# Another order of the forty attention steps in the even mixer of a two-layer diffusion backbone

## The reference, cut to what matters

```python
# MLA, each of 8 heads:          p = softmax((qn kn^T + qr kr^T) * scale);  o = p v
# differential, each of 4 heads: p = softmax(q1 k1^T * s) - lam * softmax(q2 k2^T * s);  o = p v
```

## Time and profile before

| | |
|---|---|
| median of 3 runs | 2596.94 us (2593.97 to 2598.43) |
| profiled execution | 2596.0 us, span 2594.3 us |
| PE busy | 2534.3 us (98% of the span) |
| VectorE, ScalarE, POOL busy | 1666.4, 1141.7 and 932.0 us |
| attention loop, first maximum to the last step's | 677.80 to 837.82 us: 160.02 us |
| PE, VectorE, ScalarE busy in it | 141.95, 119.97 and 102.69 us |

### The profile page before, as it was taken

How to read it: one execution, slowest core, us unless ns; L and a number is a source line. 1 busy time by engine, 2 the same in 40 slices (tenths; PEclk the granted TensorE clock), 3 DMA queues, 4 the chain that set the end, 5 groups by cost and what they waited for, 6 DMA issues and landing times. The chain is left out here.

```text
span 2594.3 us, 44719 instructions
## 1 busy us (share of the span) xinstructions
PE 2534.3 (98%) x18549; PEld 2433.6 (94%) x18549; DVE 1666.4 (64%) x2596; ACT 1141.7 (44%) x1939; POOL 932.0 (36%) x646
## 2 busy tenths in 40 slices
PE   6999999999988999999999999999999999999999
PEld 5999999999766999999999999999999999999998
DVE  5865757524677677576767757676464557757484
ACT  5442424442666454333446433344432546434253
POOL 2432434443200344334344433434332224443342
PEclk8999999999999999999999999999999999999999
DMA  7334434321100223434322343432312112232222
GB/s 272 129 131 148 143 135 142 106 91 52 60 1 1 98 66 130 147 101 169 122 82 82 130 147 102 168 121 74 101 53 72 56 46 69 66 95 69 82 78 78
DMA packets 204048, 260.35 MB, mean 100 GB/s; under 512 B 4932, under 2 KB 158152, under 8 KB 203848
## 3 DMA queue, kind: packets, MB, share of 16 engines
q1 hardware_dynamic: 203176, 254.88, 29.5%
q10 hardware_dynamic: 672, 2.62, 0.3%
HBM read 253.66 MB, written 3.82 MB: 99 GB/s over the span
## 5 line engine op out<-in xcount | busy, mean ns | idle before, releaser
L2406 POOL TENSOR_TENSOR wl<-raw,wh 128x512 fp32r<-128x512 f32 x324 | 471.4, 1485 | 705.0 <-ACT wh L2496 602.2
L2496 ACT CAST wh<-raw 128x2048 fp32r<-128x2048 f32 (+1 forms) x102 | 174.0, 1706 | 318.1 <-PE psU L3167 277.1
L2435 POOL TENSOR_TENSOR wl<-wsum,wh 128x512 fp32r<-128x512 f32 x72 | 94.1, 1306 | 363.7 <-ACT wh L2572 363.7
L2837 DVE SCALAR_TENSOR_TENSOR x<-psG,hgate,x 128x128 f32<-128x128 f32 (+1 forms) x232 | 88.4, 435 | 167.0 <-PE psG L3167 167.0
L3287 PE MATMUL psG<-sum_h,wh 128*128 128x320 f32 x576 | 178.8, 310 | 1.1
L3290 PE MATMUL psG<-sum_h,wl 128*128 128x320 f32 x576 | 177.6, 308 | 0.0
L3289 PE MATMUL psU<-sum_l,wh 128*128 128x320 f32 x576 | 177.6, 308 | 0.0
L3290 PE MATMUL psU<-sum_h,wl 128*128 128x320 f32 x576 | 177.6, 308 | 0.0
L3289 PE MATMUL psG<-sum_l,wh 128*128 128x320 f32 x576 | 177.6, 308 | 0.0
L3287 PE MATMUL psU<-sum_h,wh 128*128 128x320 f32 x576 | 177.5, 308 | 0.0
L2431 POOL TENSOR_TENSOR wl<-raw,wh 128x512 fp32r<-128x512 f32 x72 | 104.4, 1450 | 202.9 <-ACT wh L2581 202.9
(11 more groups left out here) (699 smaller groups left out, 7651.8 us busy)
## 6 DMA issues: line engine op xcount, KB each, us to landing
mraw<-in_mod_w SPq DMA_DIRECT2D x64, 1024.0 KB, 7.2
raw<-in_ffn_w_gate SPq DMA_DIRECT2D x44, 1024.0 KB, 5.1
raw<-in_ffn_w_up SPq DMA_DIRECT2D x44, 1024.0 KB, 5.1
raw<-in_ffn_w_down SPq DMA_DIRECT2D x48, 768.0 KB, 4.4
raw<-in_odd_w_in SPq DMA_DIRECT2D x12, 1024.0 KB, 5.1
raw<-in_even_w_in SPq DMA_DIRECT2D x9, 1024.0 KB, 5.1
raw<-in_ffn_w_down SPq DMA_DIRECT2D x8, 1024.0 KB, 4.9
mscale<-in_mod_w SPq DMA_DIRECT2D x4, 1024.0 KB, 10.7
```

What stands on the lines that cost most here:

```text
L2406: ins = nc.gpsimd.tensor_tensor(wl[:, slot, piece], raw[:, slot, piece], wh[:, slot, piece].bitcast(F32), ALU.subtract)
L2435: nc.gpsimd.tensor_tensor(part1(f, wl, 3), part1(f, wsum, 3), part1(f, wh, 3).bitcast(F32), ALU.subtract).then_inc(block_plo, 1)
L2496: nc.scalar.copy(wh[:, slot, 0:width], raw[:, slot, 0:width]).then_inc(w_hi, 1)
L2837: ins = nc.vector.scalar_tensor_tensor(out=xt, in0=src, scalar=hg_of(i * 2 + m, c), in1=xt, op0=ALU.mult, op1=ALU.add)
```

## The change

The function group gives the order of the ten steps of one i. Its new order keeps each long step's place among its kind, and puts the two context steps of each i between long steps:

- i = 0: D0 A0 D1 A1 D4 A2 D2 A4 D3 A3
- i = 1 and 2: A0 D4 A1 D0 A2 D1 A4 D2 A3 D3
- i = 3: A0 D4 A1 D0 A4 D1 A2 D2 A3 D3

Everything that hangs on the order (places of key halves, of casts and squares, counts for semaphores) is worked out from SEQ by the same code as before. The last four steps are the same.

```diff
@@ -499,8 +499,11 @@
 
     def group(i):
         lat, dif = [("A", i, j) for j in range(5)], [("D", i, j) for j in range(5)]
-        firsts = [x for j in range(4) for x in ((lat[j], dif[j]) if i else (dif[j], lat[j]))]
-        return [lat[4], dif[4]] + firsts if i == H_B - 1 else firsts + [lat[4], dif[4]]
+        if i == 0:
+            return [dif[0], lat[0], dif[1], lat[1], dif[4], lat[2], dif[2], lat[4], dif[3], lat[3]]
+        if i == H_B - 1:
+            return [lat[0], dif[4], lat[1], dif[0], lat[4], dif[1], lat[2], dif[2], lat[3], dif[3]]
+        return [lat[0], dif[4], lat[1], dif[0], lat[2], dif[1], lat[4], dif[2], lat[3], dif[3]]
 
     SEQ = [x for i in range(H_B) for x in group(i)]
     NS = len(SEQ)
```

## The result

The changed kernel takes 2603.47 us (median of 20 runs, 2598.90 to 2606.41), the old one beside it on the same chip 2597.28 (20 runs, 2593.70 to 2598.58). The ratio is 1.0023, with the interval 1.0017 to 1.0029: slower by 6.2 us, between 4.4 and 7.5, or 0.17 to 0.29%. The profiled execution of the changed kernel took 2599.86 us with a span of 2598.2.

The account below looks back on a forecast made before the run. No engine is full: PE, VectorE and ScalarE hand one another work in fixed order. Distances between row maxima, M(D0.1) to M(D3.3), summed to 153.75 us against 148.25, 5.5 more, so 2602.4 from 2596.94; range 2597.5 to 2606.5.

Parts of the forecast that it names:

- step 2: Long A to long D: 7 times at 4.63 us (32.41), twice after a key half (A1.3, A2.3) at 5.02 (10.04).
- step 5: Short A to long D: 3.52 us for A3.4, and 4.02 each for A0.4, A1.4 and A2.4 behind a key half.
- step 6: Four distances from A0.3 on, where long A0.3 and A1.0 meet: 4.44, 4.58, 4.23 and 4.98 us, together 18.23.
- step 1: Long D to the next A: 14 times at 4.01 us, together 56.14, set by VectorE.
- step 3: Long A to short D: 3.77 us twice (A2.0, A3.0), and 4.16 for A0.1 after its key half.
- step 4: Short D to long A: 3.03 us for D0.4; 3.31 each for D2.4 and D3.4, VectorE's scaling meeting POOL's subtraction.
- the meeting: Place where long A0.3 and A1.0, two steps of one kind, now follow each other; four distances, 18.23 us.
- Hidden after all: Rival, 25 in 100: key halves and six squares land in PE's idle time; up to 3 us more, 2597 to 2600.
- Faster: Rival, 5 in 100: a long neighbour's work covers a short step's hand-overs; A step near 2.2 us, time 2591.
- Dearer: Rival, 9 in 100: exponentials stay late through A1.1 and its D, POOL hits a third place; 2605 to 2607 us.

Follow-up runs that it names:

- e2: Changed kernel, with POOL's subtraction for head pairs 1 and 2 waiting until four more steps' maps are done; 2599.97 us against 2595.89 for the old kernel.
- e3: Changed kernel, with the short A one place earlier in i = 1 and 2, ahead of the key halves; 2608.99 us against 2595.89 for the old kernel.
- e10: Changed kernel, with PE weighing the values of every short step four times over; 2604.42 us, ratio 1.0032 to the old kernel.
- e4: Changed kernel, with ScalarE copying A1.0's first-map squares only after D1.4's exponentials; 2602.37 us in one execution against 2595.89 for the old kernel.
- e1: Changed kernel, with A0.4 and A0.3 exchanged so that short A0.4 meets long A1.0; 2601.29 us in one execution against 2595.89 for the old kernel.
- e8: Changed kernel with three edits at once, those of e1, e4 and e2; 2601.45 us in one execution against 2598.02 for the old kernel.
- e11: Changed kernel, with PE making the scores of each short A four times over; 2603.68 us, ratio 1.0029 to the old kernel.
- e9: e6 with PE weighing the values of every short step four times over; 2596.76 us, ratio 0.9999 to the old kernel.
- e7: Old kernel, with ScalarE making D0.4's exponentials ahead of the copy of A0.4's first map; 2596.18 us against 2598.02, ratio 0.9995.
- e6: e5 with ScalarE making D3.0's exponentials ahead of the copy of A3.0's first map; 2595.89 us, ratio 0.9995 to the old kernel.
- e5: Old kernel in a third order: D first in every i, short steps together, last in i = 0, 1, 2 and first in i = 3; 2598.67 us, ratio 1.0006.

## Why the prediction was right, and where it was off

The mechanism is the one that the prediction named: the changed loop costs the neighbours' work in front of each hand-over. Predicted was a stretch of 153.75, measured 153.22; a time of 2602.4, measured 2603.47. The result, 0.23%, lies just above the 0.2% that I took for the bound, and its interval reaches below it, so which side it falls on isn't settled. The stretch came out 0.53 under the sum: 0.80 too much in step 2, and some 0.3 too little in steps 5 and 6.

**Steps 1, 3, 4 and 5 hold.** Long D to A is 4.01, long A to a short D 3.76 twice and 4.16 (3.77 and 4.16 predicted), D0.4 3.01 (3.03), D2.4 and D3.4 3.32 (3.31, where the three terms shown add up to 3.29), A3.4 3.52 (3.52), the short A's behind a key half 4.06 (4.02). POOL's part is shown by e2. In D2.4 the scaling came 0.51 behind POOL's start and ended with POOL's instruction. The Trainium skill (SBUF — State Buffer, "SBUF: two separate sides") says that the one that comes second on the shared port pair waits for the other's whole instruction; the trace agrees in the main, 1.11 for a scaling that takes 0.28 alone, though only 0.08 of it lies behind POOL's recorded end, so by the records not all of its 0.28 waited. The dearer case of that rule, 1.54 for a hit just behind POOL's start, did not come up here.

**Step 2 was mis-sized in one term.** For A1.3 and A2.3 I took 5.02, the distance behind a key half in the old order. It is 4.62. There PE weighs the step before last behind the scores, and in the new order that is a short A with 4 products instead of 20:

```profile
...
756.44 0.81 DVE L991 TENSOR_REDUCE stat<-psG 128x1 f32<-128x640 f32 x1
...
758.25 0.20 PEld L1265 LDWEIGHTS psB<-pt,va 128*64 128x64 f32 x4 [0.17 <-issue]
...
761.06 0.82 DVE L991 TENSOR_REDUCE stat<-psG 128x1 f32<-128x640 f32 x1 [1.04 <-PE psU L1233]
...
```

(Order of time of the changed kernel, M(A1.3), the weighing and M(D1.3).) Loads of 0.20 stand where 1.07 stood, so the key half is absorbed. e3 is the test: with the short A's weighing in that place the step takes 4.62, with a long one's 5.03; and in e10, where the short A's four products were done four times, it takes 4.81 and 4.80. The term was 0.8 too dear in all; it is the one place where a short step hid a key half. By kind of step, the eight short steps cost 29.79 in the changed kernel against 21.40 before, and the fifteen long A's 67.27 against 70.71.

**Step 6** gave 18.23 and measured 18.42. Its one miss is D1.4, 4.23 predicted and 4.45 measured: PE begins to weigh 0.71 behind M(D1.4) (727.01 − 726.30), where I had 0.51 from a place with no squares of a long A left to turn. From there to the exponential it is 1.84 (1.82 predicted), and from that to M(A1.1) 1.90 (1.90). The cause, a wait at the head of ScalarE's queue, is shown by e4, and the meeting's part by e1.

**The rivals.** *Hidden after all* is wrong in its main term: the three short A's behind a key half took 4.06, not 3.5. It is right about the two long A's. *Faster* is wrong: no short step came near 2.2. *Dearer* is wrong about the loop: no short D has a third hit by POOL, and the delay ends with A1.1 (4.97; D1.0 has 4.01 again).

**What stays open.** The medians differ by 6.2, the stretches by 5.0, which lies within the interval of 4.4 to 7.5. A fall of the clock in the loop, which the prediction named as a sign of being wrong, doesn't show in the changed kernel's own profile. A fall at A3.4 in other executions would fit: of the eight profiles that keep the changed order there, three have one (e3, e8, e10). But e11 has no fall in its profile and came no lower, and a profile shows one execution, not the median's. What lies behind M(D3.3) varies by as much again: 1753.2 to 1758.0 us over the eight profiles of the changed kernel and its variants (e1 to e4, e8, e10, e11), and 1753.7 to 1757.4 over the other five, the old order and D first, so a loss outside the loop doesn't stand out from that spread. In e11, the longest, the clock was 0.89, 0.93 and 0.93 at 877 to 893, 1813 to 1837 and 2109 to 2133 us, and in e2, the shortest, 1.00 at all three. So the extra microsecond, if there is one, has no shown cause.

## What to carry to other kernels

The price of a step in a pipelined loop isn't its own work: write down, for each queue, what stands ahead of each hand-over, and price a new order neighbour by neighbour; that came within 0.5 us over 37 steps here. A short step doesn't cover a long one unless the long work that it replaces stood on the chain, and a copy that waits at the head of an engine's queue delays everything behind it, so put what the chain needs first. Undo the edit in parts before you believe a total, and time the best reorder against the old kernel: e9's loop is 2.75 us shorter in its profile, and the kernel isn't faster.

## What the runs showed of the hardware that I had not expected

TensorE's granted clock fell between its levels, 1.00 (2.4 GHz) to 0.50 (1.2 GHz), in the midst of the loop, behind steps in which PE worked but thinly. In the changed kernel, ahead of A3.4:

```profile
817.83:821.84 4.01, 2.04 (x13) 1.47 (x14) 3.60 (x8) 2.41 (x7) 0.00 (x0) 1.00 0.01 2
```

PE is busy for 2.04 of 4.01 us and the clock holds, while e3, e8 and e10 have a fall at the same place, with PE busy there for 2.05, 2.03 and 2.71 us. At A3.0 in the old order the clock held in the old kernel's profile and fell in e7's. So how thinly PE works ahead doesn't settle by itself whether the clock falls. A fall costs 1.5 to 2.8 us there (A3.4 at 5.03, 5.08 and 6.34 against 3.52), and in e6's stretch 4.0 (149.48 against e9's 145.50).

The loop's first two steps, D0.0 and A0.0, show the same, and stand alike in every order: M(D0.0) to M(D0.1) took 10.54, about 11.8, 12.8 (e7) or about 14.3, and the mean clock in the stretch around them goes with it. The stretches view of e5, the changed kernel and e11, in that order:

```profile
676.00:692.00 16.00, 12.05 (x67) 8.27 (x64) 13.06 (x23) 10.94 (x23) 5.34 (x4) 1.00 0.20 67
```

```profile
676.00:692.00 16.00, 12.50 (x63) 8.69 (x60) 11.92 (x20) 10.17 (x22) 5.34 (x4) 0.89 0.19 66
```

```profile
676.00:692.00 16.00, 12.58 (x44) 7.68 (x45) 10.21 (x17) 8.94 (x17) 5.34 (x4) 0.70 0.21 67
```

That is up to 3.8 us between two executions for the same work, more than half of what the change did, so a single execution's time says little about an edit of this size; the distances of the stretch, read where the clock stood at 1.00, say more.
